# Differential attention: the sums of squares of q and k as two short-form products of a split square

## The reference

```python
def _rms_norm(x, g=None, eps=1e-6):
    xf = x.astype(jnp.float32)
    y = xf * lax.rsqrt(jnp.mean(xf * xf, axis=-1, keepdims=True) + eps)
    ...
def _diff_attention(h, pos, cid, w_in, qk_norm, lam, subln, lambda_init, rel_bias):
    q, k, v = jnp.split(h @ w_in, [2 * A_HEADS * A_HD, 4 * A_HEADS * A_HD], axis=-1)
    q = _rms_norm(q.reshape(bsz, t, A_HEADS, 2, A_HD), qk_norm[0])
    k = _rms_norm(k.reshape(bsz, t, A_HEADS, 2, A_HD), qk_norm[1])
    ...
        logits = jnp.einsum("bqhmd,bkhmd->bmhqk", qb, k).astype(jnp.float32) * scale + bias
        p = jax.nn.softmax(jnp.where(visible, logits, NEG_INF), axis=-1)
        pd = p[:, 0] - lam_full * p[:, 1]
        return jnp.einsum("bhqk,bkhe->bqhe", pd.astype(v.dtype), v)
```

## Time and profile before

| | before |
|---|---|
| median of the runs | 1688.99 us |
| profiled execution, its own time | 1689.13 us |
| span of the profiled execution | 1687.3 us |
| TensorE busy | 1668.0 us, 99% of the span |
| VectorE busy | 944.0 us, 56% |
| ScalarE busy | 839.7 us, 50% |
| GpSimd busy | 737.7 us, 44% |
| granted TensorE clock in all 40 slices | 9 tenths or more |

### The profile page before, as it was taken

How to read it: one execution, slowest core, us unless ns; L and a number is a source line. 1 busy time by engine, 2 the same in 40 slices (tenths; PEclk the granted TensorE clock), 3 DMA queues, 4 the chain that set the end, 5 groups by cost and what they waited for, 6 DMA issues and landing times.

```text
span 1687.3 us, 34367 instructions
## 1 busy us (share of the span) xinstructions
PE 1668.0 (99%) x13457; PEld 1631.9 (97%) x13457; DVE 944.0 (56%) x1188; ACT 839.7 (50%) x1167; POOL 737.7 (44%) x488
## 2 busy tenths in 40 slices
PE   8999999999999999999999999999999999999999
PEld 7999999999999999999999899999999989899999
DVE  6785556534655556555466755455555557565543
ACT  7344454455544544443476644444445347654442
POOL 5135544354555445543332355533554525145520
PEclk9999999999999999999999999999999999999999
DMA  8568877543877756676642466766667732256673
GB/s 236 155 174 233 230 189 206 151 134 89 229 219 201 205 142 177 173 198 173 176 119 82 125 175 174 201 173 173 176 174 190 181 92 73 78 155 194 177 212 110
DMA packets 538690, 283.57 MB, mean 168 GB/s; under 512 B 12345, under 2 KB 532912, under 8 KB 538608
## 3 DMA queue, kind: packets, MB, share of 16 engines
q1 hardware_dynamic: 537696, 281.06, 60.9%
q0 software_dynamic: 848, 1.33, 0.4%
q10 hardware_dynamic: 64, 0.02, 0.0%
HBM read 281.29 MB, written 5.53 MB: 170 GB/s over the span
## 4 chain that ended last, share of the span: by engine, by line
PE 83%; DVE 5%; ACT 5%; DMA 3%; issue 2%; POOL 1%; SPq 0%; ACTq 0%; POOLq 0%; DVEq 0%
PE bank L1711 25%; PE bank L1713 24%; PE bank L1712 24%; DVE w_lo L1190 3%; ACT w_hi L754 2%; PE bank L2129 2%; PE bank L1755 1%; DMA raw<-in_ffn_wi 1%; DMA raw<-in_w_down 1%; DVE xg_lo L1201 1%; DMA raw<-in_w_up 1%; PE bank L2164 1%; POOL up L632 1%; PE bank L2092 1%; PE bank L1962 0%
## 5 line engine op out<-in xcount | busy, mean ns | idle before, releaser
L1711 PE MATMUL bank<-xg_hi,w_hi 128*128 128x256 f32 (+1 forms) x2504 | 719.1, 287 | 2.9 <-DVE w_lo L1190 2.9
L1713 PE MATMUL bank<-xg_hi,w_lo 128*128 128x256 f32 (+1 forms) x2504 | 714.0, 285 | 0.0
L1712 PE MATMUL bank<-xg_lo,w_hi 128*128 128x256 f32 (+1 forms) x2504 | 713.4, 285 | 0.0
L1190 DVE TENSOR_TENSOR w_lo<-raw,w_hi 128x2048 fp32r<-128x2048 f32 (+3 forms) x199 | 496.2, 2493 | 270.6 <-ACT w_hi L754 270.4
L754 ACT ACTIVATE w_hi<-raw 128x2048 fp32r<-128x2048 f32 (+3 forms) x212 | 442.0, 2085 | 264.8 <-PE bank L1713 252.2
L1711 PEld LDWEIGHTS bank<-xg_hi,w_hi 128*128 128x128 f32 x2504 | 472.3, 189 | 5.8 <-issue 4.2
L1713 PEld LDWEIGHTS bank<-xg_hi,w_lo 128*128 128x128 f32 x2504 | 472.5, 189 | 0.0
L1712 PEld LDWEIGHTS bank<-xg_lo,w_hi 128*128 128x128 f32 x2504 | 470.9, 188 | 0.7
L632 POOL TENSOR_TENSOR up<-gate,up 128x256 f32<-128x256 f32 (+1 forms) x132 | 304.3, 2305 | 252.9 <-ACT gate L1113 252.8
L1711 PE MATMUL bank<-act_hi,w_hi 128*128 128x256 f32 (+1 forms) x1056 | 301.0, 285 | 0.6 <-DVE w_lo L1190 0.4
L1712 PE MATMUL bank<-act_lo,w_hi 128*128 128x256 f32 (+1 forms) x1056 | 300.3, 284 | 0.0
(11 more groups left out here) (338 smaller groups left out, 1928.8 us busy)
## 6 DMA issues: line engine op xcount, KB each, us to landing
raw<-in_ffn_wi SPq DMA_DIRECT2D x176, 512.0 KB, 5.0
raw<-in_ffn_wo SPq DMA_DIRECT2D x32, 1408.0 KB, 7.1
raw<-in_w_gate SPq DMA_DIRECT2D x44, 512.0 KB, 4.0
raw<-in_w_up SPq DMA_DIRECT2D x44, 512.0 KB, 5.2
raw<-in_w_down SPq DMA_DIRECT2D x16, 1408.0 KB, 7.1
raw<-in_a_w_in SPq DMA_DIRECT2D x24, 512.0 KB, 5.4
raw<-in_a_in SPq DMA_DIRECT2D x20, 512.0 KB, 5.8
raw<-in_w_o SPq DMA_DIRECT2D x16, 512.0 KB, 4.7
```

The costliest lines, as they stand in the source:

```text
L1190: v.tensor_tensor(w_lo[slot][:, 0:n], raw[slot][:, 0:n], w_hi[slot][:, 0:n].bitcast(F32), ALU.subtract).then_inc(rest_ready, 1)
L1711: mm(to, lhsT=w_hi[slot][:, w], rhs=hi[:, k, cols], start=start and i == 0, stop=False)
L1712: mm(to, lhsT=w_hi[slot][:, w], rhs=lo[:, k, cols], start=False, stop=False)
L1713: ins = mm(to, lhsT=w_lo[slot][:, w], rhs=hi[:, k, cols], start=False, stop=stop and i == len(order) - 1)
```

## The change

The squares `asq` are split into a high part in the short form, by ScalarE right behind the square, and a low part, by VectorE in the place where it waits for the exponentials. TensorE then multiplies a short-form copy of `halves` by each part, four matmuls for each head where there were two in plain float32. The copy of `halves` is made by GpSimd at the start of the stage. ScalarE waits for its own square before it makes the high part; VectorE waits for the high part; TensorE waits for the low part.

```diff
+            asq_hi, asq_lo = (sb(n, [P, 2, TOK], F32R, ph) for n in ("asq_hi", "asq_lo"))
+            halves_r = sb("halves_r", [P, P], F32R, ph)
...
             gp.wait_ge(weights_used, st["diff"].first)
+            gp.tensor_copy(halves_r[:, :], halves[:, :])
             gp.memset(apt0[:, :], 0.0)
...
                     if i < 8:
                         act.wait_ge(parts_read, 2 * mixer_order(st["diff"], i) + 2)
+                        if i:
+                            act.wait_ge(a_sq_lo, i)
+                            act.wait_ge(a_sums, i)
                         act.activation(asq[:, :, :], aqkv[:, i % 2, 0:2, :], ACT.Square).then_inc(a_sq, 1)
+                        act.wait_ge(a_sq, i + 1)
+                        act.activation(asq_hi[:, :, :], asq[:, :, :], ACT.Copy).then_inc(a_sq_hi, 1)
...
                     take_part(1)
+                    if i < 8:
+                        if i:
+                            v.wait_ge(a_sums, i)
+                        v.wait_ge(a_sq_hi, i + 1)
+                        v.tensor_tensor(asq_lo[:, :, :], asq[:, :, :], asq_hi[:, :, :].bitcast(F32), ALU.subtract).then_inc(a_sq_lo, 1)
                     if 0 <= h < 8:
                         v.wait_ge(a_exp, h + 1)
...
                 def sums():
-                    pe.wait_ge(a_sq, h + 1)
+                    pe.wait_ge(a_sq_lo, h + 1)
                     if h:
                         pe.wait_ge(a_max, h)
+                    else:
+                        pe.wait_ge(a_padded, 1)
                     for m in range(2):
-                        ins = mm(bank[:, 6 + m, 0:TOK], lhsT=halves[:, :], rhs=asq[:, m, :], start=True, stop=True)
+                        mm(bank[:, 6 + m, 0:TOK], lhsT=halves_r[:, :], rhs=asq_hi[:, m, :], start=True, stop=False)
+                        ins = mm(bank[:, 6 + m, 0:TOK], lhsT=halves_r[:, :], rhs=asq_lo[:, m, :], start=False, stop=True)
                     ins.then_inc(a_sums, 1)
```

More of the change, by code:

```diff
@@ L250, in two_blocks @@
         b_sq, b_sums, b_rq, b_logits, b_max, b_exp = (sem(n) for n in ("b_sq", "b_sums", "b_rq", "b_logits", "b_max", "b_exp"))
-        a_padded, b_padded = sem("a_padded"), sem("b_padded")
+        a_padded, b_padded, a_sq_hi, a_sq_lo = sem("a_padded"), sem("b_padded"), sem("a_sq_hi"), sem("a_sq_lo")
         b_p, b_turned, b_pt, b_o = (sem(n) for n in ("b_p", "b_turned", "b_pt", "b_o"))
```

## The result

| | before | changed |
|---|---|---|
| median of 20 runs | 1689.06 us | 1692.82 us |
| lowest to highest | 1688.1 to 1691.33 | 1690.2 to 1693.79 |
| ratio, 95% interval | | 1.0019, 1.0012 to 1.0025 |
| span of the profiled execution | 1687.3 us | 1691.9 us |
| executions with mean granted clock 1.0 / 0.999 | | 6 / 14, medians 1690.98 / 1693.09 us |

The change makes the kernel slower by 0.19%, some 3.2 us by the ratio and 3.8 us by the medians. The forecast was 1691.2 us, +2.2. The median of 1692.82 us is inside the range of 8 in 10 (1687.6 to 1693.0), but above the forecast's own range (1690.6 to 1692.1). By the ratio the difference stays just under the 0.2% that I called no change; the median by itself is over the mark of 1692.4 that I had set for slower. The last row of the table holds the part that I did not foresee.

The account below looks back on a forecast made before the run. TensorE looked like the bound, with a ScalarE and VectorE loop nearly as tight; -0.42 + 4.76 - 2.10 = +2.24 us gave a forecast median of 1691.2 us. Own range 1690.6 to 1692.1; 8 in 10, 1687.6 to 1693.0.

Parts of the forecast that it names:

- rival B: Differential attention: ScalarE's step costs 0.84 us or more, so slower; 1692.8 us at the upper bound of 0.90; chance 0.18.
- The bound: Differential attention: a ScalarE and VectorE loop needs 13.50 us of the 13.77 us period, with real slack of 0.36 us.
- TensorE's products: Sums of squares: two float32 products of 0.92 us become four short-form ones of 0.50 us, gaining 0.42 us a head.
- ScalarE's high part: Between square and exponentials: a 0.64 us copy adds 0.68 us to the loop, bounds 0.55 and 0.90.
- The page's figure for it: Skill's activation budget, about 0.3 us plus 0.83 ns an element: 0.75 us for 544 elements, sum some 0.6 us larger.
- VectorE's low part: Subtraction on VectorE: 0.71 us, bounds 0.6 and 1.5, hidden in the wait for exponentials in steps 1 to 7.
- TensorE's waits: TensorE waits about 0.75 us at logits in heads 3 to 5, and about 1.2 us for head 7's low part.
- GpSimd's copy: Copy of `halves` at the stage's start: under 1.5 us, could slow VectorE's last operand by 0 to 0.3, taken as 0.
- The sum: At the stage's end: -0.42 + 4.76 - 2.10 = +2.24 us.
- Nothing is given back: Behind the stage: the 5.41 us transfer starts when TensorE frees the slot, so all the lateness moves along.
- A: Rival: the high part is covered and TensorE keeps its gain of 3.3 us, giving 1685.7 us; chance 0.16.
- C: Rival: four short-form products cost 0.92 us like the two before, giving 1691.6 us; chance 0.06.

Follow-up runs that it names:

- experiment 1: Changed kernel with only ScalarE's high part added, read by nobody, sums in plain float32; against the kernel before: ratio 1.0019, stage +2.7 us without the low clock.
- experiment 2: Changed kernel with the square written straight into the short form and multiplied twice, no low part; against the kernel before: ratio 0.9982, stage -2.52 us.
- experiment 4: Changed kernel with VectorE's low part of the output (`y_lo`) moved behind the take of k; against the kernel before: stage -0.80 us, ratio 0.9999.
- experiment 6: Changed kernel with both parts of the split made on VectorE and `y_lo` moved; against the kernel before: stage -2.83 us, ratio 0.9985.
- experiment 3: Only VectorE's subtraction of 544 columns added, result unread, sums in plain float32; against the kernel before: stage 0.00 us, ratio 1.0001.
- experiment 7: Changed kernel with the high part made by a second square of the same input, not a copy; against the kernel before: ratio 1.0011, median +2.1 us.
- the repeat: The changed kernel run again unaltered on a third chip; against the kernel before: ratio 1.0015, median +2.8 us, stage +2.29 us.

## Why the prediction was right, and what it lacked

The mechanism was right, and the sum was right for the stage. That the median of the whole program fell into the range of 8 in 10 is in part luck: the upper end of 1693.0 was set for rival B, a dearer step on ScalarE, which did not come; what lifted the median above 1692.1 was the clock, for which the prediction had no term.

- **The bound.** Right: a loop of ScalarE and VectorE lay 0.36 us a head behind TensorE. Experiments 1, 2 and 4 show it from three sides: lengthen it, shorten TensorE, shorten the loop elsewhere. The period of a head, 14.11 us, is the one that the loop gives.
- **TensorE's products.** Right, 0.42 us a head (experiment 6). In the changed kernel's timeline the four matmuls of a head follow each other after 0.12 to 0.13 us, here the last two of head 7 and the next product:
```profile
926.19 0.29 PE L1962 MATMUL bank<-asq_hi,halves_r 128*128 128x272 f32 x1
926.32 0.29 PE L1963 MATMUL bank<-asq_lo,halves_r 128*128 128x272 f32 x1
926.44 0.29 PE L1724 MATMUL bank<-y_hi,w_hi 128*128 128x272 f32 x1
```
- **ScalarE's high part.** Forecast 0.64 us for the copy and 0.68 us on the loop, measured 0.66 and 0.69. That no row showed such a copy was wrong. The trace of the kernel before has one, in a later stage, and reading it would have given the size without the estimate:
```profile
1384.34 0.66 ACT L986 ACTIVATE ckn_hi<-ckn 128x544 fp32r<-128x544 f32 x1 [0.38 <-DVE ckn L1493]
```
- **The page's figure for it.** The row of the Trainium skill (ScalarE: Activation LUTs, Rules for kernel authors) that the prediction drew on gives its 0.3 us for an activation whose bias is a pointer operand. The exponentials of line 952 have such a bias, and for 144 columns the row makes an estimate of 0.42 us, where the trace shows 0.40. The square and the copy are given no bias, so the 0.75 us did not apply to them, and their 0.66 us do not contradict it. Put into the prediction's sum in place of 0.64 us, 0.75 would also have added 7 x 0.11 = 0.8 us and not 0.6.
- **VectorE's low part.** Forecast 0.71 us and hidden; measured 0.73 and hidden (experiment 3, a stage of the same length).
- **TensorE's waits.** Right in kind: up to 0.7 us at the logits of the middle heads, 1.0 us for head 7's low part and 1.1 us for head 6's probabilities, where about 1.2 us was forecast for each; at head 1 the sums start some 0.1 us late, where 0.2 was forecast.
- **GpSimd's copy** took 0.50 us, and no row shows that it disturbed anything: VectorE's last operand beside it takes 0.70 us as before.
- **The sum.** +2.24 forecast, +2.27 measured, at the end of the stage. (The forecast's own range is called that of the copy; 1692.1 comes out of a step of 0.8 us on the loop, and a step of 0.6 us gives 1690.7 and not 1690.6.)
- **"Nothing is given back" behind the stage.** True, but incomplete. The sum had no term for the granted clock. In 14 of 20 executions the mean clock was 0.999 and not 1.0, and their median is 2.1 us above that of the other six; the profiled one of them spent 3.4 us at 1.2 GHz behind the stage. The difference of the medians is 1.5 us above what the stage accounts for. That the change makes these drops more frequent is not shown: the repeat has 5 of 11, and the kernel before has up to 14 of 33. What sets them off stays open.
- **The rivals.** A is refuted by experiment 1. B by the trace (0.69 us) and by experiment 7. C by experiments 2 and 6.

## What to carry to other kernels

An engine that is busy for half of the time can still be on a loop as tight as the bound: follow one period from an instruction back to itself over all engines, add up what is back to back, and compare with the period before putting work on it. Only an idle gap that ends with an engine outside the loop is slack; a gap in which VectorE waits for ScalarE is room for VectorE's work and for nobody else's. Here that room took both halves of the split, and the same split then gained 2.6 us in the stage where it had lost 2.3.

## What the runs showed of the hardware

- A copy of 128x544 float32 from SBUF to the short form took 0.66 us on ScalarE and 0.44 us on VectorE, 0.50 us for 128x128 on GpSimd.
- The granted clock fell to 0.50 for 3.4 us behind TensorE waits of 1.2 and 0.4 us in a row, at a cost of some 1.6 us (an estimate from that stretch), and did not fall behind 1.0 and 0.4 us. The waits' length alone does not tell: behind 1.1 and 0.6 us it fell in experiment 7 and did not in the changed kernel. Executions of one kernel differ in it (14 of 20 below 1.0), so medians a few us apart need the clock of each execution beside them.
- A wait for ScalarE's own last instruction cost 0.12 us, from start to start of two instructions of 544 columns (0.69 against 0.57).
